# Decoder block on one core: four more rows of the modulation's third segment are added in front of the rotation of the keys, and the next four are asked for in front of their doubling

## What is computed

```
mod = silu(c) @ ada_w + ada_b                  # ada_w: 2048 x 12288
sh_a, sc_a, g_a, sh_f, sc_f, g_f = split(mod, 6)
h = rms_norm(x, attn_pre_g) * (1 + sc_a) + sh_a
proj = h @ w_in                                # queries, 3 pairs of keys/values, gates, latents
...
k = apply_rope(kv[branch].keys, positions)     # rotation of the first 16 of 64 columns
k_cmp = gelu(blocks(k) @ cmp_w1 + b1) @ cmp_w2 # blocks of 32 tokens, the same for values
...
x = x + g_a * rms_norm(y, attn_post_g)         # g_a is the third segment of mod
```

## Time and profile before

| | us |
|---|---|
| median of 3 runs (2255.27 to 2260.36) | 2257.05 |
| profiled execution, device time | 2255.97 |
| its span from first to last instruction | 2254.2 |
| TensorE busy, share of the span | 87% |
| DMA, mean over the span | 366 GB/s |
| share of `ada_w` transfers in the chain that ended last | 5% |

### The profile page before, as it was taken

How to read it: one execution, slowest core, us unless ns; L and a number is a source line. 1 busy time by engine, 2 the same in 40 slices (tenths; PEclk the granted TensorE clock), 3 DMA queues, 4 the chain that set the end, 5 groups by cost and what they waited for, 6 DMA issues and landing times.

```text
span 2254.2 us, 16048 instructions
## 1 busy us (share of the span) xinstructions
PE 1958.4 (87%) x5235; PEld 913.7 (41%) x5235; DVE 1152.9 (51%) x2051; ACT 369.9 (16%) x961; POOL 765.8 (34%) x692
## 2 busy tenths in 40 slices
PE   3889899999999989999989898998687778778777
PEld 2445564444444434555434333443233333333233
DVE  6737355660310347867644345435655564755642
ACT  2001011111221114334201012101111101101101
POOL 4313000110000026556622234225544554454460
PEclk7899789999999999999999999999888889889788
DMA  9978858985569799999999999999999999999995
GB/s 362 380 282 308 293 211 306 334 318 166 165 243 345 247 373 421 421 421 421 419 418 417 418 417 420 417 417 421 421 422 422 421 420 422 422 422 422 415 422 234
DMA packets 164056, 825.44 MB, mean 366 GB/s; under 512 B 17156, under 2 KB 23528, under 8 KB 88724
## 3 DMA queue, kind: packets, MB, share of 16 engines
q0 software_dynamic: 92160, 637.58, 69.0%
q1 hardware_dynamic: 70084, 186.28, 23.1%
q10 hardware_dynamic: 1744, 0.73, 0.1%
HBM read 822.40 MB, written 2.13 MB: 366 GB/s over the span
## 4 chain that ended last, share of the span: by engine, by line
PE 49%; DMA 40%; DVE 5%; issue 3%; POOL 3%; ACT 1%; SPq 0%; DVEq 0%; POOLq 0%; ACTq 0%
DMA arena<-in_peer_v_dram,idx_now 14%; PE PS L1050 13%; PE PS L1485 9%; PE PS L1527 9%; PE PS L1442 8%; DMA arena<-in_peer_u_dram,idx_now 7%; DMA arena<-in_ada_w_dram 5%; DMA arena<-in_w_out_dram 4%; DMA arena<-in_peer_w_q_dram 3%; DMA arena<-in_w_branch_mla_dram 3%; POOL arena L590 2%; DMA arena<-in_w_branch_nsa_dram 2%; DVE arena L1579 2%; PE PS L1224 1%; PE PS L1412 1%
## 5 line engine op out<-in xcount | busy, mean ns | idle before, releaser
L1527 PE MATMUL PS<-arena 128*128 128x512 f32 x1024 | 493.7, 646 | 143.8 <-DMA arena<-in_peer_v_dram,idx_now 143.8
L590 POOL DMA_INDIRECT arena<-in_peer_v_dram,idx_now x256 | 360.7, 1409 | 590.6 <-PE PS L1485 338.0
L1485 PE MATMUL PS<-arena 128*128 128x512 f32 x1024 | 470.1, 603 | 30.7 <-DMA arena<-in_peer_v_dram,idx_now 27.6
L2074 DVE CUSTOM_DVE_ANT_0 arena<-arena 128x2048 f32<-128x2048 f32 x128 | 291.8, 2292 | 244.1 <-DMA arena<-in_peer_u_dram,idx_now 244.0
L2048 DVE CUSTOM_DVE_ANT_0 arena<-arena 128x2048 f32<-128x2048 f32 x128 | 292.7, 2291 | 195.6 <-DMA arena<-in_peer_u_dram,idx_now 193.1
L1527 PEld LDWEIGHTS PS<-arena 128*128 128x128 f32 x1024 | 210.8, 209 | 426.7 <-issue 413.6
L1050 PE MATMUL PS<-arena 128*128 128x512 f32 (+1 forms) x848 | 371.1, 591 | 0.2 <-ACT arena L695 0.2
L590 POOL DMA_INDIRECT arena<-in_peer_u_dram,idx_now x256 | 298.6, 1166 | 152.4 <-issue 72.7
L1442 PE MATMUL PS<-arena 128*128 128x512 f32 x688 | 320.0, 603 | 32.9 <-DMA arena<-in_w_out_dram 13.5
L1485 PEld LDWEIGHTS PS<-arena 128*128 128x128 f32 x1024 | 190.7, 192 | 263.2 <-issue 218.7
L1050 PEld LDWEIGHTS PS<-arena 128*128 128x128 f32 x848 | 159.1, 193 | 176.1 <-issue 168.1
(11 more groups left out here) (258 smaller groups left out, 1171.9 us busy)
## 6 DMA issues: line engine op xcount, KB each, us to landing
arena<-in_ada_w_dram POOLq DMA_DIRECT2D x64, 1024.0 KB, 7.4
arena<-in_w_in_dram SPq DMA_DIRECT2D x112, 512.0 KB, 6.2
arena<-in_ada_w_dram POOLq DMA_DIRECT2D x64, 512.0 KB, 10.5
arena<-in_w_out_dram SPq DMA_DIRECT2D x64, 512.0 KB, 5.5
arena<-in_peer_w_q_dram SPq DMA_DIRECT2D x64, 512.0 KB, 5.2
arena<-in_w_branch_nsa_dram SPq DMA_DIRECT2D x32, 512.0 KB, 6.8
arena<-in_w_branch_mla_dram SPq DMA_DIRECT2D x32, 512.0 KB, 7.1
arena<-mod_rows SPq DMA_DIRECT2D x7, 1024.0 KB, 16.5
```

Source lines behind the costliest of these rows:

```text
L590: pool.indirect_dma_start(dst, None, tab, bass.IndirectOffsetOnAxis(ap=idx_now[:, now, e:e + 1], axis=0)).then_inc(landed, 16)
L1485: ins = nc.tensor.matmul(PS[:, k, :], diag[i % 8], Vrow0[i % RING0][:, k * NC:(k + 1) * NC], start=(i == 0), stop=False, skip_group_check= ...
L1527: ins = nc.tensor.matmul(PS[:, 4 + k, :], diag[e % 8], Vrow[e % RING][:, k * NC:(k + 1) * NC], start=(first and e == 0), stop=False, skip_ ...
L2074: v.tensor_tensor_reduce(row, row, h2[1], 1.0, 0.0, ALU.mult, ALU.add, dots[:, e:e + 1]).then_inc(u_free, 1)
```

## The change

On VectorE the loop over rows 0 to 7 is cut in two: rows 0 to 3 are now added before the wait for the sines and for the first keys, rows 4 to 7 stay after the third rotation. On GpSimd the requests for rows 4 to 7 move in front of the wait for the first rotation and its doubling, and the requests for rows 8 to 11 move in front of the second doubling. The set of operations is the same, and so is each request's own condition.

```diff
@@ gpsimd @@
-            for r in range(4):
+            for r in range(8):
                 ada_row(r)
             pool.wait_ge(rope_ready, 1)
...
-            for r in range(4, 8):
+            for r in range(8, 12):
                 ada_row(r)
             pool.wait_ge(rope_ready, 3)
...
-            for r in range(8, 4 * KD):
+            for r in range(12, 4 * KD):
                 ada_row(r)
@@ vector @@
+            for r in range(4):
+                ada_row(r)
             dve.wait_ge(sin_ready, 2)
             dve.wait_ge(pj_out, 1)
             rope(KV0, GROUPS, rope_ready)
...
-            for r in range(8):
+            for r in range(4, 8):
                 ada_row(r)
```

## The result

| | before | changed |
|---|---|---|
| median, us | 2256.19 (6 runs, 2255.14 to 2260.36) | 2240.51 (6 runs, 2237.08 to 2246.41) |
| profiled execution, us | 2255.97 | 2246.41 |
| from the first product of the compression (L1124) to the product at L1135, us | 60.32 | 42.90 |

The ratio is 0.9929, with a 95% interval of 0.9915 to 0.9943: 16 us faster, between 13 and 19. The forecast was 2240.0; that it is within 0.5 us of the median is closer than an interval 6 us wide can claim, so the exact hit is luck. The profiled execution of the changed kernel happens to be the slowest of its six, so its span (2244.7 us) must not be set against that of before; the stretch that the change touches can.

The account below looks back on a forecast made before the run. TensorE bounds, waiting in the compression for `cmp_w1` tiles starved by row transfers. Waits 8.3, half-clock tiles 6.9, 0.9 and 1.3 behind, less 0.3, give 17.1 us: 2255.97 becomes 2238.9, as median 2240.0; range 2236 to 2251.

Parts of the forecast that it names:

- The bound: Compression on TensorE: late `cmp_w1` tiles, q1 getting 45 GB/s beside q0's 348; 29.7 us instead of 14.5.
- The additions in front of the rotations: VectorE, idle from 143.4 to 170.6: rows 0 to 3 take 8.6 us, end at about 152, cost nothing.
- The requests: GpSimd: rows 4 to 7 asked for from 144.7 to 152.1, rows 12 to 17 from 201.5 to 213.7.
- Tiles in time: Compression: `cmp_w1` tiles 43 to 47 land from 222.8 to 229.4, before TensorE wants them, by 1.6 to 2.3 us.
- The sum: Compression 14.5 us, column sums 1.06, C5 27.63: the next product, at 279.30 before, starts 17.1 us earlier.
- It lasts to the end: Behind the compression: everything starts from the shifted point, so the whole 17.1 us is kept to the end.
- the prediction's own sign of being wrong: After C5: a difference of 17 us at 262 that is smaller at 450 or at 840.
- The clock didn't fall without a wait: Rival in the compression: the clock falls though nothing waits, 9.1 us of the gain go, 2249.1 us; chance 0.13.
- The remaining wait: Rival in the compression: tile 43 lands 2.4 us late; 2242.4 us, or 2253.2 if the clock falls; chance 0.14.
- The absorbed gain: Rival in the later stream of rows: TensorE's 5.31 us wait grows by what was won, 2257 us; chance 0.08.
- the starved tile 42: Rival in the compression: contention takes in tile 42, waits start two tiles earlier, 3.4 us more, 2260.5 us; chance 0.05.

Follow-up runs that it names:

- two spare transfers: Changed kernel with two more 1 MB transfers on GpSimd's queue, behind the requests for rows 12 and 13, to a buffer nothing reads; 2255.41 us.
- the 4 KB runs: Kernel before with only `cmp_w1` read differently, one 4 KB run per partition instead of four of 1 KB; 2248.54 us.
- eight early, and used: Changed kernel with rows 0 to 7 before the rotations, column sums inside the compression, rows 16 to 19 added meanwhile, two fewer left for attention; 2244.49 us.
- only the requests moved: Kernel before with only GpSimd's requests moved earlier, VectorE adding rows 0 to 7 behind the rotations as before; 2251.94 us.

## Why the prediction was right

*The bound.* Named rightly, and shown by two opposite interventions: bigger packets on q1 without moving a row end the waits for `cmp_w1`, and spare bytes on q0 with all rows moved bring them back.

*The additions in front of the rotations.* Predicted 143.4 to 152 at no cost; they run from 141.77 to 150.45 in a profile that is 1.5 us ahead there and 1.9 us ahead from the rotations on. The rotations begin when the sines come, as before, and the first doubling starts 1.98 us earlier, the shift of that profile alone.

*The requests.* Predicted 144.7 to 152.1 for rows 4 to 7, 201.5 to 213.7 for rows 12 to 17; seen 143.35 to 150.74 and 199.83 to 212.10, which with the shift is within 0.4 us. Row 15 is added 1.2 us later than predicted (at 217.8, with the shift 219.7, against 218.5).

*Tiles in time.* The step that I trusted least, by a margin of 1.6 to 2.3 us, held in all three profiles, with 1.3 us as the least; two spare rows broke it. With the shift of 1.9 us, tiles 44 to 47 land within 0.6 us of the predicted times. Tile 43 lands 4.5 us earlier than predicted: q1 got 54 GB/s beside the rows from 206 to 218 us (647 packets, 0.64 MB) and not the 45 that I had carried over. That error sat where there was room to spare, so it cost the forecast nothing.

*The sum.* 17.1 us from the first thin product to L1135; seen 60.32 - 42.90 = 17.42. The terms: compression 14.40 (14.5), column sums 1.06 (1.06), C5 27.73 (27.63).

*It lasts to the end.* 17.1 us predicted, 16 measured, with an interval of 13 to 19. The single profiles don't show it so cleanly, and the prediction's own sign of being wrong, a difference that is smaller at 450 or at 840, did appear in the first pair: 19.4 us at L1135 had become 17.2 at the column sums of the fifth segment, by the later wait, 11.9 at the first product of L1485 (at 839.5 us in the kernel before) and 9.6 at the end. But the other two profiles of the changed kernel, 21.9 and 18.9 us ahead at L1135, are 25.6 and 17.8 ahead at L1485 and 25.3 and 17.6 in span; the second profile of before goes from 1.8 ahead to 0.7 behind and 1.9 behind. So up to 840 us the lead wanders by some microseconds either way, in both kernels; from there on it is kept within 2.4 us in all of them. The medians carry the reading, not one pair of profiles; what makes the wandering stays open.

*The rivals.* The clock didn't fall without a wait: 14.40 us of thin products at 1.00. The remaining wait didn't come, but its price list was right in kind: two spare transfers give a 2.4 us wait with the clock falling behind it, and five tiles at half, as that rival had it; that rival had put the gain left at 3.9 us, and the kernel with two spare transfers has 3.5 (2255.41 beside a before of 2258.88). The absorbed gain and the starved tile 42 didn't occur. I had not named one bound: row 15, which stood 0.7 us behind the compression in the kernel before. It didn't matter, as the change moves it too, but it made the expectation for the 4 KB runs wrong.

## What to carry to other kernels

When a wait names a small transfer, look at what the other queue carries at the time and in what packets: long runs on one queue starve short runs on the other, and the cure may be to move the large transfers to where the engines stand half idle, by freeing their slots earlier. Count a short wait of TensorE in front of thin products at a multiple of its length (here 8.3 us of waits cost 17.4, and 2.4 us cost 13.7). And read behind the first bound for the second before pricing a cure of the first alone.

## What the runs showed of the hardware

- Where both queues were busy they moved about as many packets each, whatever the packets held: 557 and 541 packets of 7.5 and 1 KB gave 348 and 45 GB/s; with 3.8 KB on q1, 481 and 403 packets gave 296 and 127 GB/s (206 to 218 us in both).
- Back-to-back products of 60 columns held the clock at 1.00 for 14.4 us (three profiles of the changed kernel), but once it was at 0.50 they didn't lift it in 17.4 us (80 records in one piece in the kernel with two spare transfers).
- The clock fell in a wait of 2.40 us between thin products (two spare transfers), and 1.4 us behind one of 1.46 us ahead of short products (eight early, and used, at 394.9). It held over one of 1.77 us behind chunk C3 (only the requests moved, up to 190.9), where C4 then took its 27.63 us.
- A late wait of one program varied between 3.1 and 7.6 us in three profiles, with the same order of instructions.
